# Begin and end of the linear-attention loop: order of the softmax combining, decay factors, weight splits and the last tile's norm

## The reference, cut to what matters

```
proj  = rms_norm(h) @ w_in                          # q, k, v, r, gates; dq, dk, dv
o_gla = rms_norm(intra(q, k, v, decay) + (q*exp(b)) @ state) * silu(r)
        state = exp(g_last) * state + (k*exp(g_last-b)).T @ v
w     = softmax(dq1 dk1 + bias) - lam * softmax(dq2 dk2 + bias)
o_dif = rms_norm(w @ dv) * (1 - lambda_init)
h     = h + concat(o_gla, o_dif) @ w_out
h     = h + experts(rms_norm(h))                    # token lists, gather, 3 products, scatter-add
```

## Time and profile before

| what | us |
|---|---|
| median of three runs | 1230.29 |
| profiled execution | 1229.69 |
| its span, first to last instruction | 1227.9 |
| TensorE busy in the span | 1150.3 (94%) |
| VectorE busy | 887.6 (72%) |
| ScalarE busy | 693.0 (56%) |
| GpSimd busy | 259.9 (21%) |
| mean granted clock of TensorE | 0.971 |

### The profile page before, as it was taken

How to read it: one execution, slowest core, us unless ns; L and a number is a source line. 1 busy time by engine, 2 the same in 40 slices (tenths; PEclk the granted TensorE clock), 3 DMA queues, 4 the chain that set the end, 5 groups by cost and what they waited for, 6 DMA issues and landing times. The chain is left out here.

```text
span 1227.9 us, 17109 instructions
## 1 busy us (share of the span) xinstructions
PE 1150.3 (94%) x5875; PEld 871.6 (71%) x5876; DVE 887.6 (72%) x1306; ACT 693.0 (56%) x913; POOL 259.9 (21%) x324
## 2 busy tenths in 40 slices
PE   5999999899999789999599999999999999999993
PEld 4877887666777568888467777777777777777772
DVE  4424423656576677886689999999999999999882
ACT  4425203454455543434257777777777777777771
POOL 2202102422121122222242212212212212212100
PEclk9998999999999889999699999999999999999997
DMA  8130201100200533352599999999999999999941
GB/s 309 44 103 1 103 21 49 69 35 26 95 26 9 172 92 141 122 184 87 183 366 375 398 376 379 396 377 377 394 374 370 395 373 374 396 378 368 397 141 26
DMA packets 67425, 273.33 MB, mean 223 GB/s; under 512 B 13156, under 2 KB 19880, under 8 KB 42664
## 3 DMA queue, kind: packets, MB, share of 16 engines
q1 hardware_dynamic: 56744, 245.32, 51.7%
q0 software_dynamic: 7168, 20.98, 7.5%
q10 hardware_dynamic: 3456, 6.29, 1.3%
HBM read 248.44 MB, written 28.32 MB: 225 GB/s over the span
## 5 line engine op out<-in xcount | busy, mean ns | idle before, releaser
L1904 DVE TENSOR_TENSOR main_w_low<-w_raw,main_w_high 128x2048 fp32r<-128x2048 f32 x190 | 434.5, 2287 | 50.3 <-ACT main_w_high L1900 49.9
L1900 ACT CAST main_w_high<-w_raw 128x2048 fp32r<-128x2048 f32 x190 | 362.2, 1908 | 73.5 <-PE main_score L1920 52.5
L1828 POOL DMA_INDIRECT main_xg<-xn_dram,main_token x32 | 75.9, 2372 | 372.9 <-DVE main_token L1808 366.1
L1918 PE MATMUL main_pt<-main_w_high,main_xT_high 128*96 128x512 f32 x256 | 103.6, 405 | 1.2 <-DVE main_xT_low L2061 1.2
L1918 PE MATMUL main_score<-main_w_high,main_hT_high 128*96 128x512 f32 x256 | 103.1, 403 | 1.2 <-DVE main_hT_low L2073 1.2
L1920 PE MATMUL main_pt<-main_w_high,main_xT_low 128*96 128x512 f32 x256 | 102.4, 400 | 0.0
L1919 PE MATMUL main_pt<-main_w_low,main_xT_high 128*96 128x512 f32 x256 | 101.5, 396 | 0.0
L1920 PE MATMUL main_po<-main_w_high,main_xT_low 128*96 128x512 f32 x256 | 101.2, 395 | 0.0
L1920 PE MATMUL main_score<-main_w_high,main_hT_low 128*96 128x512 f32 x256 | 101.2, 395 | 0.0
L1919 PE MATMUL main_score<-main_w_low,main_hT_high 128*96 128x512 f32 x256 | 101.1, 395 | 0.0
L1918 PE MATMUL main_po<-main_w_high,main_xT_high 128*96 128x512 f32 x256 | 100.7, 393 | 0.0
(11 more groups left out here) (307 smaller groups left out, 2312.2 us busy)
## 6 DMA issues: line engine op xcount, KB each, us to landing
w_raw<-in_moe_w SPq DMA_DIRECT2D x192, 1024.0 KB, 18.0
slot_raw<-in_w_in SPq DMA_DIRECT2D x12, 1024.0 KB, 7.4
main_x<-in_x SPq DMA_DIRECT2D x8, 512.0 KB, 11.0
slot_raw<-in_w_out SPq DMA_DIRECT2D x4, 1024.0 KB, 6.7
main_hx<-in_x SPq DMA_DIRECT2D x8, 512.0 KB, 3.9
out<-main_hx SPq DMA_DIRECT2D x8, 512.0 KB, 2.9
xn_dram<-main_xn SPq DMA_DIRECT2D x8, 512.0 KB, 2.8
gr_dram<-main_stage ACTq DMA_DIRECT2D x8, 256.0 KB, 2.0
```

Source lines behind the costliest of these rows:

```text
L1828: nc.gpsimd.indirect_dma_start(xg[u][:], None, s["xn2_dram"], bass.IndirectOffsetOnAxis(token[u][:, 0:1], 0), bounds_check=bound["x"], oob ...
L1900: nc.scalar.copy(wh[slot(c, e)][:], raw[u][c // 2][:, c % 2, :]).then_inc(w_high, 1)
L1904: nc.vector.tensor_tensor(wl[slot(c, e)][:], raw[u][c // 2][:, c % 2, :], wh[slot(c, e)][:].bitcast(F32), ALU.subtract).then_inc(w_low, 1)
L1918: nc.tensor.matmul(out, x_hi, w_hi, start=start, stop=False)
```

## The change

It moves instructions in the hand-written lists and adds none.

- Step m = N-1 of the softmax items loses `make_factors(0)` on ScalarE and `exponents(0)` with the clearing of `sc` and `state` on VectorE; they stand in step N, behind `turned_high("d", 0)` and `turned_low("d", 0)`.
- On VectorE the split of chunk 7's first half (`weight_low(7, 0)`) and the scaling of the second norm's gain and the router's weights move from ahead of tile loop n = 1 to places inside it, behind `turned_low("g", 0)` and behind `turned_low("d", 1)`.
- On TensorE `turn("g", 7)` moves from the begin of iteration 8 to the end of iteration 7, ahead of `router(6)`.
- On ScalarE `first_high(act, 0)` moves from the end of iteration 7 to ahead of its `route_exps(5)`. On VectorE `first_low(dve, 0)` now stands ahead of `position(5)`, `g_sum(7)` ahead of `h_norm(6)`, and `logits(6)` behind `turned_low("g", 7)`.

```diff
--- before.py
+++ after.py
@@ -908,8 +908,8 @@
         for n in range(1, T + 1):
             if n == 1:
                 inner(n)
-            turn("g", n - 1)
             if n < T:
+                turn("g", n - 1)
                 if n > 1:
                     inner(n)
                 turn("d", n)
@@ -924,6 +924,8 @@
                 if n >= 2:
                     count(n - 2)
                 out_products(n, "d")
+            if n == T - 1:
+                turn("g", n)
             router(n - 1)
         count(T - 1)
 
@@ -1133,10 +1135,9 @@
                     spill(i)
             if m in split_at:
                 weight_high(*split_at[m])
-            if m == N - 1:
-                make_factors(0)
             if m == N:
                 turned_high("d", 0)
+                make_factors(0)
             if m == N + 1:
                 inner(0)
             if m >= 2:
@@ -1153,6 +1154,8 @@
                 turned_high("d", n)
                 if n + 1 < T:
                     make_factors(n + 1)
+                else:
+                    first_high(act, 0)
             if n >= 2:
                 route_exps(n - 2)
             if n < T:
@@ -1162,8 +1165,7 @@
                 for half in range(2):
                     store_hxT(n - 1, half)
                 if n == T - 1:
-                    for c in range(2):
-                        first_high(act, c)
+                    first_high(act, 1)
             else:
                 for half in range(2):
                     h_square(n - 1, half)
@@ -1636,14 +1638,13 @@
                     q_sum(i)
             if m in split_at:
                 weight_low(*split_at[m])
-            if m == N - 1:
-                exponents(0)
-                dve_then(dve, nc.vector.memset(sc[:], 0.0))
-                nc.vector.memset(state[:], 0.0).then_inc(state_ready, 1)
             if m >= N:
                 norm(m - 3)
             if m == N:
                 turned_low("d", 0)
+                exponents(0)
+                dve_then(dve, nc.vector.memset(sc[:], 0.0))
+                nc.vector.memset(state[:], 0.0).then_inc(state_ready, 1)
                 scale_qk(0)
                 weight_low(7, 1)
         mask(0)
@@ -1653,21 +1654,24 @@
         g_sum(0)
         scale_qk(1)
         g_norm(0)
-        weight_low(7, 0)
-        dve.wait_ge(g2_in, 16)
-
-        dve_then(dve, nc.vector.tensor_scalar(g2[:], g2[:], D ** 0.5, None, ALU.mult))
-        dve.wait_ge(router_in, 16 * (4 + KD))
-        nc.vector.scalar_tensor_tensor(out=wr[:], in0=wr[:], scalar=D ** 0.5,
-                                       in1=g2T[:].unsqueeze(2).to_broadcast([P, KD, NG + NE]), op0=ALU.mult,
-                                       op1=ALU.mult).then_inc(prepared, 1)
         for n in range(1, T + 1):
             turned_low("g", n - 1)
+            if n == 1:
+                weight_low(7, 0)
             if n < T:
                 mask(n)
                 turned_low("d", n)
+                if n == 1:
+                    dve.wait_ge(g2_in, 16)
+                    dve_then(dve, nc.vector.tensor_scalar(g2[:], g2[:], D ** 0.5, None, ALU.mult))
+                    dve.wait_ge(router_in, 16 * (4 + KD))
+                    nc.vector.scalar_tensor_tensor(out=wr[:], in0=wr[:], scalar=D ** 0.5,
+                                                   in1=g2T[:].unsqueeze(2).to_broadcast([P, KD, NG + NE]),
+                                                   op0=ALU.mult, op1=ALU.mult).then_inc(prepared, 1)
                 if n + 1 < T:
                     exponents(n + 1)
+            if n == T:
+                logits(n - 2)
             if n >= 2:
                 route(n - 2)
             if n == T:
@@ -1681,17 +1685,21 @@
                     scale_qk(n + 1)
                 if n + 1 < T:
                     carry(n)
+                else:
+                    first_low(dve, 0)
                 if n >= 2:
                     position(n - 2)
-                if n == T - 1:
-                    first_low(dve, 0)
+            if n == T - 1:
+                g_sum(n)
             h_norm(n - 1)
             if n < T:
-                g_sum(n)
+                if n < T - 1:
+                    g_sum(n)
                 g_norm(n)
                 if n >= 2:
                     shares(dve, n - 2)
-            logits(n - 1)
+            if n != T - 1:
+                logits(n - 1)
         route(T - 1)
         last_positions()
```

## The result

The changed kernel took 1213.67 us by the median of four runs (1212.22 to 1215.12), the kernel before 1229.67 in its runs beside it. The ratio is 0.9876, 95% interval 0.986 to 0.9892: faster by 16 us, or 1.2%. The profiled execution took 1213.02, its span is 1211.2 (before: 1227.9) and its mean granted clock 0.982 (before: 0.971).

A forecast was written before the change was run, and what follows sets the result against it. TensorE bounds the kernel, so only its waits before tile 1 and between tile 7 and the first expert count. Begin 8.0 plus tile 7 7.7 is 15.7, less 0.3 for latencies, from 1229.69: 1214.3 us, range 1211.5 to 1220.5.

The forecast's parts named there:

- First step: Begin, item 30 ahead of the first decay tile: TensorE's 6.37 us wait falls under 1.5, 4.3 us gained.
- Second step: Begin, weight splits behind turned tile 0: products start 6.3 us earlier, at full clock; with the First step 8.0 us.
- Tile 7: Last tile: earlier expert split, turn ahead of router(6), tile 6's norm during GpSimd's root; last addition 7.7 us sooner.
- To the first expert: From tile 7 to the experts: the same chain, only shifted; first gate product near 599.3 (it was 614.9).
- Rival (a): Clock falls at begin (6.0 instead of 8.0), tile 7 (5.3 instead of 7.7) or both (1218.7); chance 0.17.
- (b): VectorE or ScalarE late by a few microseconds at either end; only 8 to 11 us remain, 1219 to 1222; chance 0.1.
- (c): Begin: item 30's copy waits for something besides program order, 6.37 us stays; 9.7 us remain, 1220; chance 0.03.
- (d): Expert stage keeps the lower clock beyond its first products; 14.5 us per expert, so the kernel ends slower; chance 0.02.
- (e): Expert stage: its stream, at DMA share 0.98, cannot follow and the gain is given back, 1229.5; chance 0.03.

The follow-up runs named there:

- second execution: The changed kernel run once more with nothing changed, as the measure for the runs beside it; 1213.44 us, ratio 0.987 to the kernel before.

## Why the prediction was right, and which steps were off

The forecast was 1214.3, measured 1213.67 (the profiled execution, against which the sum was made: 1213.02). The sum was 15.7 less 0.3; the span shows 16.7.

- **First step, 4.3.** By this step outer(0) falls at 433.7 and came at 433.77; item 31's values, foreseen at 431.75, came at 431.88. That this fits so well is half luck, since two errors met. The working had item 30's values at the full clock, and they ran at the lower one, so that item 31's second copy ended last (431.83). And it made the chain over ScalarE too long: in the changed kernel's second execution, at the full clock and with the same start as before, item 30's square ended at 426.22 (foreseen 426.9), the weight's low half at 430.50 (431.3) and the norm at 430.76 (431.7). There the values started at 430.92, and the step is 5.17:

```profile
430.92 2.02 PE L726 MATMUL main_po<-dv,main_wT 128*128 128x128 f32 x16 [0.99 <-DVE dqT L1400]
```

- **Second step, both together 8.0.** Products at 444.46 (foreseen 444.35), outer(1) at 450.04 (449.95), turn of tile 1 at 461.15 (461.3 to 461.6). The split was covered; VectorE's chain became last, at a cost of 0.47. Begin: 8.3 to 8.5 with the first step at 4.35, over 9 where it is 5.17.
- **Tile 7, 7.7: the step that was off.** Measured 6.70. The range covers it. The mis-sized term is the 1.2 us of tile 6's norm, which I took off the chain because it "now runs while GpSimd works out tile 7's root". It runs beside it, but holds it: L1238 took 1.14 instead of 0.24, and 0.9 of the 1.2 came back. The norm ended 0.9 late, so did the products (574.70; the forecast, moved by the begin's shift of 8.3, had 573.8) and all behind them. The rest held: the split started when outer(7) ended, router(6) covered both halves, and the additions were in time. The norm of h stood there in the prediction with its row, but I costed it as VectorE's time alone and didn't ask what it and GpSimd share.
- **To the first expert.** First gate product 600.13, foreseen near 599.3: the 1.0 of tile 7 and 0.26 behind it, less what the begin gave more.
- **The clock.** Both groups of products held 1.00, as forecast. Rival (a) is nonetheless real: it showed at tile 0 in three other profiles (2.0 net, as priced) and at tile 7 in one (1.6). The Trainium skill's rule that I set against the row ("TensorE: Matmul & The Clock Gate", "A second HAM failure mode: psum-queue depth-cycling") is borne out to that extent: groups of matmuls with waits of 0.5 to 1.1 us between them sometimes lose the clock here, and sometimes not, with the same code. What decides between the two stays open. The row with 1.21 of 2.00 us busy at 1.00 did not rule it out.
- **What came on top.** 1.56 us of the 16.7 are the last down products, 0.3 the first gate products, both the clock of the single execution. Without them the profiled gain is 14.8, under the forecast's 15.4: tile 7's term came out 1.0 short, the begin's 0.3 to 0.5 over. So the last 0.6 us between forecast and median is no proof of the sum: errors of about 1 us in single terms cancelled. The medians (16.0 here, 15.9 in the second execution's job) average over such states.
- **The other rivals.** (b): the additions and the split were in time; the stretches that they guard are the same in both profiles of the changed kernel (7.63 at tile 0, 8.72 and 8.71 at tile 7). (c): the wait of 6.37 went, as program order said. (d) and (e): the expert stage took 566.25 to 566.30 in all profiles.

## What to carry to other kernels

When a move places one engine's instruction beside another's, ask whether the two share a way to memory: overlap in time is not yet free. Three small GpSimd operations grew here beside a two-input VectorE operation, from 0.24 to 1.14, from 0.29 to 2.47 and, untested, from 0.57 to 1.58 us. A wait of several microseconds ahead of a long group of matmuls costs its length and then about as much again at the lower clock, so a removed wait can be worth twice its size (3.4 and 3.2 us for one weight split). Add up parts by their stretches and not by medians: the stretches of the parts gave 16.0 as the whole did, while their medians, each uncertain by 1 to 3 us, gave 19. And compare executions by stretches between fixed instructions; single spans carried up to 1.6 us of clock at the last products and 7 us of a different start.

## What the runs showed of the hardware that was not expected

- The granted clock differs between executions at the same instruction after the same wait, in one program or in kernels with the same code ahead of it: item 30's values 3.65 or 2.02 us (wait 1.0), the last down products 7.28 or 8.84 (wait 1.16), router(7) 2.92 or 1.98 (wait 0.87), and 2.90 or 2.12 (waits 1.17 and 1.18).
- Twenty transposes in a wait of 4.8 us cut it to 0.55 and 0.33. They ran at the lower clock themselves, and the first expert's products behind them held the full clock in one execution and not in the other.
- GpSimd's short operations ended just behind VectorE's instruction: L1238 at 569.87, VectorE's norm of h at 569.77; L493 at 603.51, the split at 603.35; L1193 at 421.63, the combining at 421.20.
